# Opening each projection with four weight tiles instead of three, with a shorter inner normalisation, in a three-layer float32 kernel

## The reference

```
h = layernorm(x, emb_ln_g, emb_ln_b)
for l in range(2):
    proj = h @ w_in[l]                       # 2048 x 4928, the 39 "in" tiles
    mix  = concat(mla, pool, conv)           # attention, pooling, convolution, gated
    out  = mix @ w_out[l] + b_out[l]         # 16 "out" tiles
    h    = layernorm(alpha * h + out, ln_g[l], ln_b[l])
n = rms_norm(h, norm_g) * (1 + scale) + shift  # second block
z = n @ w_in_2                               # first 8 tiles: v, then u, then g_a
...
```

## Time and profile before

| what | value |
|---|---|
| time, median of 3 runs | 2435.57 us (2435.48 to 2437.75) |
| the profiled execution: its own time, its span | 2436.52 us, 2434.9 us |
| PE busy | 2377.6 us, 98% of the span |
| DVE busy | 1267.6 us, 52% |
| ACT busy | 877.3 us, 36% |
| POOL busy | 395.6 us, 16% |
| chain that ended last | PE 88%, DVE 6%, ACT 2%, issue 2% |

### The profile page before, as it was taken

One profiled execution on the slowest core, in us unless ns is written; L12 is line 12 of the kernel. 1 busy time (PEld: TensorE's weight loads), 2 busy tenths in 40 slices (PEclk: granted clock), 3 DMA queues, 4 the chain that ended last, 5 costly groups with the idle time before them and its releaser, 6 DMA issues.

```text
span 2434.9 us, 31642 instructions
## 1 busy us (share of the span) xinstructions
PE 2377.6 (98%) x11538; PEld 1964.1 (81%) x11538; DVE 1267.6 (52%) x1870; ACT 877.3 (36%) x1327; POOL 395.6 (16%) x388
## 2 busy tenths in 40 slices
PE   6999999999999999999999999999999999999998
PEld 5888888888887888888788887788878888887887
DVE  8655543466547556443466767552264444444334
ACT  5422222465225322223365223422234444444221
POOL 0300000033114200000032113112002222222000
PEclk9999999999999999999999999999999999999999
DMA  6555553212332555553212232423222222223332
GB/s 232 194 182 179 175 180 112 78 53 70 103 97 67 187 174 171 184 169 129 78 53 78 86 103 95 159 87 107 96 78 78 78 78 78 78 69 124 109 103 78
DMA packets 80906, 281.91 MB, mean 116 GB/s; under 512 B 8896, under 2 KB 13248, under 8 KB 79936
## 3 DMA queue, kind: packets, MB, share of 16 engines
q1 hardware_dynamic: 63968, 217.49, 27.2%
q0 software_dynamic: 16864, 63.45, 7.6%
HBM read 272.51 MB, written 8.39 MB: 115 GB/s over the span
## 4 chain that ended last, share of the span: by engine, by line
PE 88%; DVE 6%; ACT 2%; issue 2%; POOL 1%; DMA 1%; SPq 0%; DVEq 0%; ACTq 0%
PE bank L342 27%; PE bank L344 27%; PE bank L343 27%; DVE w_lo L336 1%; DVE x_lo L1149 1%; PE bank L2104 1%; POOL probs L423 1%; PE bank L2027 1%; ACT w_hi L313 1%; DMA w_raw<-stream 1%; DVE x_res L1109 0%; PE bank L2184 0%; PE bank L1864 0%; PE bank L1865 0%; PE bank L2185 0%
## 5 line engine op out<-in xcount | busy, mean ns | idle before, releaser
L344 PE MATMUL bank<-x_hi,w_hi 128*128 128x512 f32 x2896 | 1126.9, 389 | 0.0
L343 PE MATMUL bank<-x_hi,w_lo 128*128 128x512 f32 x2896 | 1124.9, 388 | 0.0
L342 PE MATMUL bank<-x_lo,w_hi 128*128 128x512 f32 (+1 forms) x2384 | 948.3, 398 | 12.5 <-DVE x_lo L1149 5.9
L336 DVE SCALAR_TENSOR_TENSOR w_lo<-w_raw,w_hi 128x1024 fp32r<-128x1024 f32 (+1 forms) x384 | 477.0, 1245 | 733.2 <-ACT w_hi L313 732.3
L313 ACT ACTIVATE w_hi<-w_raw 128x1024 fp32r<-128x1024 f32 x390 | 408.1, 1048 | 951.3 <-PE bank L344 913.6
L344 PEld LDWEIGHTS bank<-x_hi,w_hi 128*128 128x128 f32 x2896 | 544.0, 188 | 114.4
L343 PEld LDWEIGHTS bank<-x_hi,w_lo 128*128 128x128 f32 x2896 | 545.2, 188 | 106.7 <-issue 2.2
L342 PEld LDWEIGHTS bank<-x_lo,w_hi 128*128 128x128 f32 x2384 | 449.4, 189 | 106.1 <-issue 6.4
L342 PE MATMUL bank<-mix_lo,w_hi 128*128 128x512 f32 (+1 forms) x656 | 255.5, 390 | 1.3 <-issue 1.0
L423 POOL TENSOR_SCALAR probs<-probs,stats 128x128 f32<-128x128 f32 (+3 forms) x128 | 138.5, 1088 | 662.5 <-DVE stats L1510 662.4
L342 PEld LDWEIGHTS bank<-mix_lo,w_hi 128*128 128x128 f32 x656 | 123.8, 189 | 26.5 <-issue 1.4
(11 more groups left out here) (330 smaller groups left out, 2205.7 us busy)
## 6 DMA issues: line engine op xcount, KB each, us to landing
w_raw<-stream SPq DMA_DIRECT2D x390, 512.0 KB, 3.4
ada_w<-wada POOLq DMA_DIRECT2D x96, 512.0 KB, 4.5
x_tokens<-xN SPq DMA_DIRECT2D x4, 1024.0 KB, 8.4
x_res<-xT SPq DMA_DIRECT2D x16, 256.0 KB, 10.8
x_res_spill<-x_res POOLq DMA_DIRECT2D x8, 512.0 KB, 6.1
x_res<-x_res_spill POOLq DMA_DIRECT2D x8, 512.0 KB, 7.4
outT<-x_res SPq DMA_DIRECT2D x16, 256.0 KB, 2.2
cond_b<-cond POOLq DMA_DIRECT2D x2, 1024.0 KB, 5.2
```

Of the source, the lines that this page charges most:

```text
L336: nc.vector.scalar_tensor_tensor(out=WL[:, slot, :cols[n]], in0=RAW[:, slot, :cols[n]], scalar=1.0, in1=WH[:, slot, :cols[n]].bitcast(F32) ...
L342: nc.tensor.matmul(out, wh, xl, start=first, stop=False)
L343: nc.tensor.matmul(out, wl, xh, start=False, stop=False)
L344: return nc.tensor.matmul(out, wh, xh, start=False, stop=last)
```

## The change

It has five parts. (1) `first_tiles` runs four tiles side by side: the eight units are now four first halves (0 to 3) and four second halves (4 to 7), rows 0 and 1 go tile by tile as their weights come, rows 2 to 4 row by row, and the rest in groups of three and then two rows per tile. (2) For the embedding, DVE no longer splits three units ahead of the first row but puts units 1, 2, 3 between the rows; SP asks for unit 3 after two feature rows, not five. (3) The units 4 to 7 are split in the row loop at rows 10 to 13 (9 to 12 in the second block), on ACT and on DVE. (4) The inner norms get the mean's broadcast from two full matmuls with `ones`, of the running sum before the last row and of the last row, in place of a diagonal matrix and a spread; two of the four diagonal blocks go to ACT; DVE subtracts the mean from rows 0 and 1 itself, and POOL starts at row 2, in the second block only when `x_lo` four rows back is written. (5) The sums of the latent norm move from tile 3 to tile 4, the fills shrink (20 to 13, 12 to 7, 12 to 2), and the four transposes of the second block are all in tile 4.

```diff
-                if k == 4:
+                if k == 1:
                     load(0, SLOTS - 1)
...
             def norm_end(n):
...
                 for k in range(KT):
-                    if n == 0 and k == 5:
+                    if n == 0 and k == 2:
                         split(0, 1, (1,))
-                    if k in (11, 12):
-                        split(n, 2, (k - 11,))
+                    if k in (10, 11, 12, 13):
+                        split(n, k // 2 - 3, (k % 2,))
...
-            def normalise(n, between={}):
+            def normalise(n):
...
-                for k in range(KT):
-                    if k in between:
-                        between[k]()
-                    by_token(n, k)
-                    if k >= 2:
-                        lo(k - 2)
-                for k in (KT - 2, KT - 1):
+                by_token(n, 0)
+                by_token(n, 1)
+                lo(0)
+                if n == 0:
+                    split(0, 0, (1,))
+                    lo(1)
+                    split(0, 1, (0,))
+                    by_token(n, 2)
+                    split(0, 1, (1,))
+                    by_token(n, 3)
+                    lo(2)
+                else:
+                    by_token(n, 2)
+                    by_token(n, 3)
+                    lo(1)
+                    split(n - 1, T_OUT + KT + 1, (1,))
+                lag = 1 if n == 0 else 2
+                for k in range(4, KT):
+                    if k in (10, 11, 12, 13):
+                        split(n, k // 2 - 3, (k % 2,))
+                    by_token(n, k)
+                    lo(k - lag)
+                for k in range(KT - lag, KT):
                     lo(k)
...
             token_stats()
-            split(0, 0)
-            split(0, 1, (0,))
+            split(0, 0, (0,))
             dve.wait_ge(S["x_bc"], 2)
-            normalise(0, {6: lambda: split(0, 1, (1,)), 13: lambda: split(0, 2, (0,)), 14: lambda: split(0, 2, (1,))})
+            normalise(0)
...
             def norm_rms_end():
...
-                    if k in (10, 11):
-                        split(B2, 2, (k - 10,))
-                    if k == 12:
-                        split(B2, 3, (0,))
+                    if k in (9, 10, 11, 12):
+                        split(B2, 2 + (k - 9) // 2, ((k - 9) % 2,))
...
             def norm_sums(n):
                 last_layer = n == DEPTH
-                fill(5)
+                pe.wait_ge(S["sum1"], KT * n - 1)
+                mm(PS[2][:, :], ONES[:, :], A1[:, :], start=True, stop=False).then_inc(S["pre_mm"], 1)
+                pe.wait_ge(S["out_ev"], KT * n)
+                mm(PS[2][:, :], ONES[:, :], Y[:, KT - 1, :], start=False, stop=True).then_inc(S["bc_m"], 1)
...
-                spread(S["dg_m"], QB * n, DG[0], 2).then_inc(S["bc_m"], 1)
...
-            def first_tiles(l, mid={}):
-
-
-                order = [(k, t) for k in range(8) for t in range(3)]
-                order += [(k, t) for t in range(3) for k in range(8, 11)]
...
+            def first_tiles(l):
+
+
+                pairs = ((0, 2), (2, 3), (3, 4)) if l == 0 else ((0, 3), (3, 4))
+                order = [(k, t) for t0, t1 in pairs for k in range(2) for t in range(t0, t1)]
+                order += [(k, t) for k in range(2, 5) for t in range(4)]
+                for k0, k1 in ((5, 8), (8, 10), (10, 12), (12, 14), (14, 16)):
+                    order += [(k, t) for t in range(4) for k in range(k0, k1)]
...
-                    in_tile(m, {T_Q + 1: {7: [lambda: lat_sums(0)], 12: [lambda: lat_bcast(0)]},
+                    in_tile(m, {T_Q + 2: {1: [lambda: lat_sums(0)], 5: [lambda: lat_bcast(0)]},
```

More of the change, by code:

```diff
@@ L407, in sub @@
                         .then_inc(S["n_sub"], 1)
-                for b in range(4):
-                    if gated and b == 1:
-                        pool.wait_ge(S["acc"], 3 * KT)
-                    if gated and b == 2:
-                        pool.wait_ge(S["r_v"], 1)
+                for b in (2, 3):
                     sub(b)
@@ L534, in root, with mean_copy @@
                 nc.scalar.activation(ST[:, 24:28], ST[:, 20:24], ACT.Sqrt, bias=ST[:, 3:4]).then_inc(S["st_sd"], 1)
+                act.wait_ge(S["st_ri"], n)
+                for t in range(2, QB):
+                    nc.scalar.activation(DG[1][:, t, :], IDN[:, :], ACT.Copy, scale=ST[:, 28 + t:29 + t])\
+                        .then_inc(S["dg_r"], 1)
+            def mean_copy(n):
                 act.wait_ge(S["bc_m"], n)
-                nc.scalar.activation(SB[:, :], PS[2][:, :], ACT.Copy).then_inc(S["sh_tot"], 1)
+                nc.scalar.activation(SB[:, :], PS[2][:, :], ACT.Copy, scale=1.0 / D).then_inc(S["sh_tot"], 1)
             def norm_end(n):
@@ L565, in norm_rms_end @@
                 nc.scalar.activation(RT[:, 8:12], RT[:, 4:8], ACT.Sqrt).then_inc(S["r_sd"], 1)
+                act.wait_ge(S["r_ri"], 1)
+                for t in range(2, QB):
+                    nc.scalar.activation(DG[0][:, t, :], IDN[:, :], ACT.Copy, scale=RT[:, 12 + t:13 + t])\
+                        .then_inc(S["r_dg"], 1)
                 whole(0)
@@ L575, in norm_rms_end @@
                         .then_inc(S["h_hi"], 1)
-                    if k + 2 < KT:
+                    if k == 1:
+                        whole(2)
+                        whole(3)
+                    if 2 <= k < KT - 2:
                         whole(k + 2)
@@ L1116, in mean_diag, with sub_mean @@
                 dve.wait_ge(S["st_v"], 3 * n - 2)
-                for t in range(QB):
-                    TS(DG[0][:, t, :], IDN[:, :], ST[:, 16 + t:17 + t], None, ALU.mult).then_inc(S["dg_m"], 1)
                 TT(out=ST[:, 28:32], in0=ST[:, 16:20], in1=ST[:, 16:20], op=ALU.mult).then_inc(S["st_v"], 1)
+            def sub_mean(n, k):
+                if k == 0:
+                    dve.wait_ge(S["sh_tot"], n)
+                TT(out=NBUF[k][:, :], in0=Y[:, k, :], in1=SB[:, :], op=ALU.subtract).then_inc(S["n_sub"], 1)
             def variance(n):
@@ L1130, in scale_diag @@
                 dve.wait_ge(S["st_ri"], n)
-                for t in range(QB):
+                for t in range(2):
                     TS(DG[1][:, t, :], IDN[:, :], ST[:, 28 + t:29 + t], None, ALU.mult).then_inc(S["dg_r"], 1)
@@ L1300, in layer @@
                     if i == 0:
-                        split(l, 3)
+                        split(l, 4, (0,))
                     if i not in (0, 2):
@@ L1557, in _ @@
                 if s < 2:
-                    split(B2, 3 + s, (0, 1) if s else (1,))
+                    split(B2, 4, (s,))
                 if s == 2:
@@ L1893, in first_tiles @@
                     half, col0 = k // 8, (k % 8) * P
-                    slot, before, _ = unit(l, 3 * half + t if t < 3 else 6 + half)
+                    slot, before, _ = unit(l, 4 * half + t)
                     if k % 8 == 0:
@@ L1901, in first_tiles @@
                         last.then_inc(w_used, 1)
-                    for j in mid.get((k, t), ()):
-                        va_trans(j)
             def layer(l):
                 def in_tile(m, mid={}, i=0):
-                    if m not in (T_KR, 3):
-                        pe.wait_ge(S["in_ev"], taken(l, m - 2) + 2 * i)
-                    tile(l, m, {T_KR: 7, 3: FIRST_BANKS[3]}.get(m, m % 2), mid=mid, i=i,
+                    if m != T_KR:
+                        pe.wait_ge(S["in_ev"], taken(l, m - (2 if m > T_KR else 4)) + 2 * i)
+                    tile(l, m, 7 if m == T_KR else m % 2, mid=mid, i=i,
                          order=LAST_ORDER if m == IN_TILES - 1 else range(KT))
@@ L2319, in pack_stream_2 @@
     units = []
-    units += first_order([tile_units(w_in, c[part] + P * m) for part in ("v", "u", "g_a") for m in range(8)])
+    units += first_order([tile_units(w_in, c[part] + P * m) for part in ("v", "u", "g_a") for m in range(8)], 4)
     f = w_in[:, c["f"]:c["f"] + B2_HEADS]
```

118 lines of the change are left out of this document (59 added, 59 removed).

## The result

The changed kernel takes 2443.28 us, the median of 9 runs (2440.58 to 2447.15); the kernel before took 2435.57 beside it. The ratio is 1.0029, 95% interval 1.0021 to 1.0038: slower by 7.7 us by the medians.

A forecast was written before the change was run, and what follows sets the result against it. PE, busy 98% of the span, was taken to bound the kernel. The terms 6.0 + 2.0 + 0.5 - 8.5 + 1.0 summed to +1.0 us over 2435.6, about 2437, range 2427 to 2445.

The forecast's parts named there:

- main case: Whole kernel: the summed terms hold, about 2437 us, reaching from 2430 to 2441; chance 0.63.
- rival B: Both layers: GpSimd's residual rows starve unit 8's w_lo, up to 3.5 us each plus half clock; 2446 to 2448; chance 0.25.
- The closed chain in layer 0: Layer 0, second halves: ACT and DVE wait on each other, 5.15 us a unit; tile 5 begins 6.0 us later.
- The wait for the tables: Layer 0, before tile 5: ACT's Sin and Silu tables, with the later broadcast, make unit 10 1.35 us late.
- The clock's term, +2.0 in layer 0: Layer 0: PE's 3.8 us stops bring a half-clock stretch, +2.0 us, between 0 and 3.4.
- Layer 1: Layer 1 opening: earlier first product, chain period 4.4 us, a half-clock stretch giving 1.7 back; in all +0.5 us.
- The term "-8.5": Second block: fewer fills and earlier rows, units 3.06 us apart; tile 5 earlier by 7.7 to 9.9 us, taken as 8.5.
- the rule that I weighed: Second block: idleness halves the clock, so cutting fills leaves the first rows at half clock; -6.3 us instead of -8.5.
- rival C: First rows of layer 1 and second block: too few fills, clock down, 2 us each at most; 2439 to 2441; chance 0.15.
- the sign that I had set: Prediction is wrong if DVE's split beside the residual rows takes over 2 us with PE waiting for it.
- the term at +1.0: Both layers: GpSimd's residual rows running beside unit 8's w_lo on DVE cost +1.0 us.
- Rival A: Openings: the chain of splits does not form or units come in time; -20 us, 2415; chance 0.12.

The follow-up runs named there:

- the profiles of the pacing and of the fills: Changed kernel with the second block's GpSimd rows released by x_res as before, 2438.85 us; changed kernel with the old fills (20, 12, 12), 2446.44 us.
- the second profile: The changed kernel once more, unedited, in one further profiled run: 2445.05 us.
- the first profile: The profiled execution among the changed kernel's nine measured runs, unedited: 2447.15 us.
- the tiles alone: Changed kernel with the inner norms, old pacing and inner fills (12 and 12) of the kernel before; four tiles and new split places kept: 2444.95 us.
- the first three repaired kernels: Changed kernel with the row ahead of the split in both layers, 2426.99 us; also old second-block pacing, 2425.75; also Sin and Silu a latent later, 2423.80.
- all four edits: Changed kernel with row ahead of split, old second-block pacing, Sin and Silu a latent later, and GpSimd's residual rows behind its ada_w loads: 2422.24 us.

## Why the prediction was right and where it was wrong

The time, 2443.3, lies in the range, but outside the main case's 2430 to 2441: I gave 0.62 to "no change that can be told" and 0.23 to slower, and it is slower, by more than the 4.9 us that I had called hard to tell. That the number is inside the range is in part luck. The range went up to 2445 for the sake of rival B, and what brought the time there was another thing, the second block, which gained 4.7 to 7.7 us less than I had taken.

**The closed chain in layer 0: right, with its numbers.** Forecast `w_lo` of the second halves done at 47.9, 53.1, 58.2, 63.4, a period of 5.15 and idle times of about 2 us on DVE; measured starts at 46.82, 51.91, 56.98, 62.06 (so done 1.2 later), 5.08 and 1.94. Tile 5 was forecast at 95.6 to 95.9, and 2.0 later with the clock. Eight profiles have this part of layer 0 as in the changed kernel or nearly so. It began at 95.2 to 96.2 in the three where the half clock cost nothing, at 97.1 to 98.2 in four where it did, and at 101.33 in the one with the collision. The wait for the tables was forecast at 1.35 and is 1.33, and its cause is shown by moving the tables.

**The clock's term, +2.0 in layer 0: right in its mechanism, and its size goes with the execution.** Dummy matmuls in the stops keep the clock up. The half clock cost 0 to 2.5 us, within the 0 to 3.4 that I gave. What came between the second and the third stop fell into the shadow of the third, which the sum did not allow for: PE's third stop was forecast at 3.8 and is 2.15. Only half clock behind the third stop cost time: from 66 to 74 the granted clock is 1.00 in the profiles of the pacing and of the fills, and 0.79 to 0.89 in those where tile 5 came later.

**Layer 1: right.** +0.7 against +0.5; first product 10.4 us after the last one of layer 0, as in the forecast (762.9 less 752.5); units 4.4 to 4.7 apart against 4.4. In the second profile the opening came 0.9 us later than in the first, since the spread ahead of it ran at half clock (1.93 us instead of 1.13).

**The second block: here a term failed.** The term "-8.5" rests on "The chain isn't closed here ...: 3.06 us a unit, the last at 1531.6 to 1533.4, stops of 0.3 and 1.7". The lists are as I read them, but the durations were those of an unhindered DVE. The change as I described it has part 4 release GpSimd's rows by `x_lo`, and I never costed it. It puts each row beside a split, 2.05 us instead of 1.21, a period of 3.9 and stops of 2.2 and 1.4 with a stretch of half clock between them. With the old pacing the period is 3.06 and the rows and tiles up to tile 5 take 60.1 us instead of 65.0 or 63.3. By the first profile the term misses 7.7 us. Of these 4.8 are the pacing. Some 1.6 are the first product, which came 16.3 us behind the last one of layer 1 and not 13.5 to 15.3. The last 1.3 lie between the 60.1 and the 58.6 to 59.0 that I had worked out, and were not split further. By the second profile of the same kernel the term misses 4.7: the pacing is 3.2 of it, and the first product came at 15.0, within the forecast, since PE's sums took 5.4 us there and 6.7 in the first, so that part is the clock of one execution. The medians give the pacing 4.4.

**The fills (the rule that I weighed, and rival C): the products did not start at half clock.** In both profiles the granted clock is 1.00 in the 5 us from the first product on, in layer 1 and in the second block; only the spread ahead of them ran at half clock. So the -6.3 of that rule and the 2 us of rival C have no place in the account, and the kernel with the old fills is slower, not faster.

**GpSimd against the split of unit 8 (rival B): right as a mechanism, and not what made the kernel slower.** By the sign that I had set, a split of over 2 us with PE waiting for it, the first profile speaks against the prediction: 4.52 us, PE waiting 2.69. But the second profile of the same kernel has 1.23, and taking the collision away moved the median by 0.4, with the term at +1.0. It cost PE 4 us in layer 0 in one profile of six. In layer 1 the same split took 1.8 us in both profiles of the changed kernel and PE did not wait for it. In other kernels PE did wait for it there: 1.57 us behind a split of 3.40 with dummy matmuls in the stops, 1.58 behind 3.42 with the tiles alone, and 0.7 to 0.8 behind 2.5 to 2.6 in the first three repaired kernels. The Trainium skill, "SBUF — State Buffer", Who interferes with whom, has the pair of ports held for a whole instruction, and the order of issue decides who blocks. The two outcomes at one place fit that. The prediction took from it that the split would lose one row, 0.7 us, and that does not fit: it lost 3.3 us, about five rows of 0.69.

**Rival A** (no chain) is out: the chain stands in every profile. Its 2415 was more than an open chain gives: with the chain opened and the pacing undone the kernel reaches 2425.8, with all four edits 2422.2.

## What to carry to other kernels

When two engines pass work back and forth, write down one round of both lists: if each has its own long job ahead of the same item, the round is the sum of both; moving the shared item ahead of the long job on one side opens it, here for 16 us. A change of what releases an off-path engine is a change of what it runs beside, and it has to be costed even when that engine is never waited for. And before an instruction on a queue that also issues loads is made to wait, look at which loads stand behind it.

## What the runs showed that I had not expected

The same split beside the same GpSimd rows took 4.52 us in one execution and 1.23 in another of the same kernel, and while DVE lost, GpSimd's 16 rows kept 11.1 us; when DVE won, they took 13.6. The changed kernel's runs spread over 6.6 us, those of the kernel before beside them over 3.3. The collision and the stretches of half clock account for swings of this size between profiles; that they are all of the spread was not tested.
